# A two-layer streaming encoder step: the dense token group becomes the third and fourth prompt chunk, and its layer-1 keys, values and queries move behind the gathered selection

## The reference

```python
# layer 0 (gMLP mixer), then PEER
h = h + gmlp_mix(rms_norm(h, norm_mix[0]), ...)
h = h + peer_ffn(rms_norm(h, norm_ffn[0]), ...)
kv = rms_norm(h, norm_kv) @ w_kv            # one shared K/V, 4 heads of 64
# layer 1 (windowed attention), then PEER
q = rms_norm(h, norm_mix[1]) @ attn_w_q     # 16 heads of 64
h = h + prompt_or_cached_window_attention(q, k, v) @ attn_w_o
h = h + peer_ffn(rms_norm(h, norm_ffn[1]), ...)
y = rms_norm(h, norm_final)
```

## Time and profile before

| | before |
|---|---|
| median of three runs | 3103.03 us |
| profiled execution, its own time | 3099.71 us |
| its span, first to last instruction | 3097.6 us |
| mean granted TensorE clock, share of full | 0.963 |
| PE busy | 2907.3 us, 94% |
| DVE busy | 2439.5 us, 79% |
| POOL busy | 1028.0 us, 33% |
| ACT busy | 797.2 us, 26% |
| chain that ended last: share of DMA, DVE, PE | 22%, 9%, 5% |

### The profile page before, as it was taken

How to read it: one execution, slowest core, us unless ns; L and a number is a source line. 1 busy time by engine, 2 the same in 40 slices (tenths; PEclk the granted TensorE clock), 3 DMA queues, 4 the chain that set the end, 5 groups by cost and what they waited for, 6 DMA issues and landing times. The chain is left out here.

```text
span 3097.6 us, 46546 instructions
## 1 busy us (share of the span) xinstructions
PE 2907.3 (94%) x17342; PEld 2551.9 (82%) x17342; DVE 2439.5 (79%) x5311; ACT 797.2 (26%) x2328; POOL 1028.0 (33%) x837
## 2 busy tenths in 40 slices
PE   8899899999999999987888979999999999999977
PEld 7898789888888888876677958789888888888856
DVE  3387899988888888877653868998888888888877
ACT  5333222221111211111454352222121221122112
POOL 5532222332233333333365311222233333333332
PEclk9999999999999999998989969989999999999999
DMA  5337889999999999999522358788999999999997
GB/s 182 116 97 288 311 318 365 389 422 422 422 422 422 413 420 413 422 410 416 206 67 83 101 206 309 291 301 335 422 422 421 421 422 419 419 412 420 409 422 292
DMA packets 159964, 1042.97 MB, mean 337 GB/s; under 512 B 18480, under 2 KB 23920, under 8 KB 44096
## 3 DMA queue, kind: packets, MB, share of 16 engines
q0 software_dynamic: 92160, 671.13, 53.0%
q1 hardware_dynamic: 63648, 357.59, 29.8%
q10 hardware_dynamic: 4000, 12.36, 1.0%
HBM read 1033.28 MB, written 7.86 MB: 336 GB/s over the span
## 5 line engine op out<-in xcount | busy, mean ns | idle before, releaser
L779 PE MATMUL bank<-a,V 128*128 128x256 f32 x4096 | 927.8, 386 | 64.4 <-DVE a L1777 56.6
L779 PEld LDWEIGHTS bank<-a,V 128*128 128x128 f32 x4096 | 791.3, 194 | 184.3 <-issue 62.4
L766 PE MATMUL bank<-xd,U 128*128 128x256 f32 x4096 | 935.2, 388 | 3.2 <-DMA U<-uvd 3.2
L1398 POOL DMA_INDIRECT gata<-uvg,idxg x428 | 512.3, 1197 | 1219.6 <-DVE acc L1794 1165.3
L766 PEld LDWEIGHTS bank<-xd,U 128*128 128x128 f32 x4096 | 786.6, 194 | 110.4 <-DMA U<-uvd 4.2
L1786 DVE CUSTOM_DVE_ANT_0 gata<-gata,xrow 128x1024 f32<-128x1024 f32 x428 | 522.6, 1221 | 218.5 <-DMA gata<-uvg,idxg 215.7
L1184 ACT ACTIVATE act<-dot 128x1 f32<-128x1 f32 x640 | 129.6, 202 | 1666.1 <-DVE dot L1786 1666.0
L1794 DVE SCALAR_TENSOR_TENSOR acc<-gata,wgt,acc 128x1024 f32<-128x1024 f32 x428 | 548.1, 1281 | 2.5 <-ACT wgt L1186 2.3
L1398 POOL DMA_INDIRECT gatb<-uvg,idxg x212 | 246.1, 1161 | 531.5 <-DVE acc L1794 521.5
L1786 DVE CUSTOM_DVE_ANT_0 gatb<-gatb,xrow 128x1024 f32<-128x1024 f32 x212 | 259.1, 1222 | 114.7 <-DMA gatb<-uvg,idxg 114.0
L753 PEld LDWEIGHTS bank<-B,oneA 128*128 128x128 f16 x4096 | 278.7, 150 | 32.7 <-issue 19.5
(11 more groups left out here) (207 smaller groups left out, 2482.4 us busy)
## 6 DMA issues: line engine op xcount, KB each, us to landing
U<-uvd SPq DMA_DIRECT2D x128, 1024.0 KB, 9.0
V<-uvd SPq DMA_DIRECT2D x128, 1024.0 KB, 9.0
raw<-lin SPq DMA_DIRECT2D x152, 512.0 KB, 3.6
gata<-uvg,idxg POOLq DMA_INDIRECT x428, 14.7
hsp<-h ACTq DMA_DIRECT2D x2, 2304.0 KB, 17.0
hx<-hsp SPq DMA_DIRECT2D x2, 2304.0 KB, 17.2
gatb<-uvg,idxg POOLq DMA_INDIRECT x212, 14.7
sk_g<-skT ACTq DMA_DIRECT2D x2, 1024.0 KB, 4.8
```

Source lines behind the costliest of these rows:

```text
L766: mm = pe.matmul(bank[s][:, TD * t:TD * t + TD], U[:, s, o:o + P], xd[:, k, :], start=(t == 0 and k == 0), stop=(k == DT - 1), skip_group_ ...
L779: mm = pe.matmul(bank[b][:, TD * (d % 2):TD * (d % 2) + TD], V[:, s, o:o + P], a[:, s, TD * k:TD * k + TD], start=(first and k == 0 and d ...
L1398: pool.indirect_dma_start(row(l, s), None, uvg[l], bass.IndirectOffsetOnAxis(idxg[:, s:s + 1], 0)).then_inc(g_in[s % SLOTS], 16)
```

## The change

On the host the prompt is rolled, so that the dense group now holds prompt tokens 256 to 511 and the gathered group prompt tokens 0 to 255 and the stream. g's attention then needs only g's keys: its chunk 2 is the first of the prompt and has one block. d's chunk 0 now follows g's chunk 3 and has two blocks, as chunk 1 has.

- All that concerns d in layer 1 ahead of its attention moves behind the gathered selection: `n3d`'s sums go behind `n3g`'s, its squares and root behind g's on ACT; the normed keys' operand (`xkv`) is made by DVE in pieces inside the selection `pq1g`; `kvd` follows `pq1g`, then the gathered index, two tiles of `qd` and d's values. The other six tiles of `qd` stand inside d's attention, after units 1, 3, 5, 7, 9 and 11 (`Q_AT`).
- d's attention writes to one PSUM bank instead of two, because the query tiles take bank 5; its results go to buffers of their own (`xo`).
- `n3g`'s scale stays in a PSUM bank, and the second apply of that norm (`mix1`, for the queries) has buffers of its own (`xf2`, `xh2`, `xl2`); it follows the first apply at once instead of waiting until `kvg` is done.
- ACT makes the four high parts of `kvg`'s weights ahead of `n3g`'s squares. The loads of the cached keys move from ACT's queue to SP's, ahead of `qg`'s weights. `kvg`'s low parts stand ahead of the activations' on POOL.
- In `AT`, the four places in d's attention take three gather steps each instead of two: `EARLY[1]` is 62, so that 42 steps instead of 46 are left for the last 16 pairs.

```diff
-    [*[(f"att{n}", 2) for n in (3, 7, 11, 16)], *[(f"add{m}", 1) for m in range(7)], ("mid1", 4),
+    [*[(f"att{n}", 3) for n in (3, 7, 11, 16)], *[(f"add{m}", 1) for m in range(7)], ("mid1", 4),
...
-LOADS = ["ing", "outg", "pq0g", "ind", "outd", "pq0d", "kvd", "kvg", "qg", "og", "pq1g", "qd", "od", "pq1d"]
+LOADS = ["ing", "outg", "pq0g", "ind", "outd", "pq0d", "kvg", "qg", "og", "pq1g", "kvd", "qd", "od", "pq1d"]
...
-IN_BANK = ("n0g", "n0d", "n1g", "n2g", "n4g")
...
+IN_BANK = ("n0g", "n0d", "n1g", "n2g", "n3g", "n4g")
...
+        Q_AT = {2 * m - 3: m for m in range(2, DT)}
...
         def keys(c):
 
-            return (P, [P]) if c == 0 else (0, [P, P]) if c < 4 else (0, [P, DEC])
+            return (P, [P]) if c == 2 else (0, [P, P]) if c < 4 else (0, [P, DEC])
+
+        def out_place(grp, n):
+
+            return (4 + n % 2, n // 2) if grp == "g" else (4, n)
...
+        def tile_bank(name, m):
+
+            if name != "qd":
+                return m % 4, BASE[name][m % 4] + m // 4
+            if m < 2:
+                return 2 + m, BASE["qd"][2 + m]
+            return 5, BASE["qx"][5] + m - 2
...
+            linear("kvg")
+            sp.wait_ge(hsum_done, DT)
+            sp.dma_start(ck[:, :, :], ckT).then_inc(attn_in, 16)
+            sp.dma_start(cvs[:, :], cv).then_inc(attn_in, 16)
+            sp.dma_start(dst[:, :], dist).then_inc(attn_in, 16)
+            sp.dma_start(snk[:, :], sinks.broadcast_to([P, HEADS])).then_inc(attn_in, 16)
...
+                if not l:
+                    norm_sums("n3d")
...
             for m in range(4):
-                tile("kvd", m, None, xd, (nv_done, DT * APPLY["kvd"]))
-            for m in range(4):
                 tile("kvg", m, "kv")
             for m in range(DT):
                 tile("qg", m, "mix1")
...
                     q = qT[grp][r, j, span(grp, c)]
-                    if c == 0:
-                        blocks = [kvs[r, j // 4, 0:P]]
+                    if c == 2:
+                        blocks = [kvs[r, j // 4, k0:k0 + P]]
+                    elif c == 0:
+                        blocks = [kvs[r, j // 4, TCO[3]:TCO[3] + P], kvs[r, j // 4, 0:P]]
...
                     if n < len(UNITS[grp]):
+                        if grp == "d" and n % 2 == 0:
+                            pe.wait_ge(*tile_out("qd", n // 2))
                         att_scores(grp, n)
                     if 0 <= n - LAG < len(UNITS[grp]):
                         att_turn(grp, n - LAG)
                     if 0 <= n - LAG - 1:
                         att_out(grp, n - LAG - 1)
-                for b in (4, 5):
-                    pe.wait_ge(free[b], BASE[f"att{grp}"][b] + len(UNITS[grp]) // 2)
+                    if grp == "d" and n in Q_AT:
+                        tile_d("qd", Q_AT[n], xd)
...
             selection(1, "g")
-            for m in range(DT):
-                tile("qd", m, None, xd, (nv_done, DT * APPLY["mix1d"]))
-                if m == 4:
-                    second_rank(1, 0)
-                if m == 5:
-                    gathered_index(1, 0, (0,))
-                if m == 6:
-                    gathered_index(1, 0, (1,))
+            for m in range(4):
+                tile_d("kvd", m, xkv, (nv_done, DT * APPLY["kvd"]))
+            second_rank(1, 0)
+            gathered_index(1, 0, (0,))
+            gathered_index(1, 0, (1,))
+            for m in range(2):
+                tile_d("qd", m, xd, (nv_done, DT * APPLY["mix1d"]))
+            values("d")
+            pe.wait_ge(vnat_done, 4)
             attention("d")
...
+                if l:
+                    root("n5d")
...
+            for m in range(4):
+                weight_high("kvg", m)
             squares_of_sums(0)
             for dt in range(DT):
-                act.wait_ge(nv_done, DT * APPLY["kvd"] + dt + 1 + (dt % 2 == 0))
-                act.activation(h[:, dt, COLS["d"]], dense_sum(dt), ACT.Copy).then_inc(dsum_done, 1)
-                if dt % 2 == 1:
-                    act.wait_ge(dsum_done, dt + 1)
-                    act.nop().then_inc(free[4 + dt // 2], 1)
-
-            act.dma_start(ck[:, :, :], ckT).then_inc(attn_in, 16)
-            act.dma_start(cvs[:, :], cv).then_inc(attn_in, 16)
-            act.dma_start(dst[:, :], dist).then_inc(attn_in, 16)
-            act.dma_start(snk[:, :], sinks.broadcast_to([P, HEADS])).then_inc(attn_in, 16)
+                square("n3d", h[:, dt, COLS["d"]], dt)
             high_parts("kv", "kvg")
...
+            root("n3d")
...
-            high_parts("mix1", "mix1g")
...
+                if m < 2:
+                    high_parts("mix1", "mix1g", range(4 * m, 4 * m + 4))
...
                 else:
-                    act.activation(xd[:, j, span(grp, c)], bank[b][:, 0:TCS[c]], ACT.Copy).then_inc(free[b], 1)
+                    act.activation(xo[j][:, span(grp, c)], bank[b][:, 0:TCS[c]], ACT.Copy).then_inc(free[b], 1)
...
                         weights_at(1, f"att{n}")
+                        if n in Q_AT:
+                            query("d", Q_AT[n])
...
-            queries("d")
+            for m in range(4):
+                act.wait_ge(*tile_done("kvd", m))
+                act.activation(kvs[:, m, COLS["d"]], bank[m][:, 0:TD], ACT.Copy).then_inc(free[m], 1)
+                if m == 2:
+                    gate_exp(1, 0)
...
+            for m in range(2):
+                query("d", m)
...
+            act.nop().then_inc(vnat_done, 1)
             attention("d")
...
+            first_lows("kvg")
             low_parts(PARTS["kv"])
-            first_lows("kvg")
-            first_lows("qg")
-            low_parts(PARTS["mix1"])
+            for m in range(4):
+                first_lows("qg", (m,))
+                if m < 2:
+                    for dt in (4 * m, 4 * m + 2):
+                        low_part(pool, PARTS["mix1"], dt, xl_done)
...
+                    elif l and 3 <= m < 3 + DT:
+                        keys_d([m - 3])
...
+                    if l and dt == 1:
+                        inverse("n5d")
+                    if l and dt >= 2:
+                        dense_out([dt - 2])
+                if l:
+                    dense_out(range(DT - 2, DT))
...
+            def keys_d(pieces):
+
+                dve.wait_ge(xr_done, 2)
+                apply(G_KV, "d", lambda dt: h[:, dt, COLS["d"]], lambda dt: xkv[:, dt, :], pieces=pieces)
...
-            normed("n3g", G_KV, "g", "kv")
-            for b in range(4):
-                dve.wait_ge(*tile_done("kvg", b))
-            normed(None, G_MIX1, "g", "mix1")
...
+            inverse("n3g")
+            of_h = lambda dt: h[:, dt, COLS["g"]]
+            apply(G_KV, "g", of_h, lambda dt: xf[:, dt, :], "kv", norm="n3g", keep=True)
+            apply(G_MIX1, "g", of_h, lambda dt: xf2[:, dt, :], "mix1", norm="n3g")
+            inverse("n3d")
...
+    x = np.concatenate([f["x_prompt"][0, TD:], f["x_prompt"][0, :TD], f["x_sample"][0]])
```

More of the change, by code:

```diff
@@ L148, in plan @@
     chosen_g(1)
-    lin("qd")
-    seg("attd", **{f"b{b}": 8 for b in range(8)})
+    lin("kvd")
+    seg("vnd", b4=1, b5=1)
+    seg("qd", b2=1, b3=1)
+    seg("qx", b5=6)
+    seg("attd", b0=8, b1=8, b2=8, b3=8, b4=16, b6=8, b7=8)
     lin("od")
@@ L403, in wait_slot @@
                 eng.wait_ge(lo_done[m % 4], LO[last] + k // 4 + 1)
-            elif name == "kvd":
+            elif name == "kvg":
                 for b in range(2):
@@ L1006, in squares_of_h, with high_parts @@
                 root(norm)
-            def high_parts(part, ap):
-                for dt in range(DT):
+            def high_parts(part, ap, pieces=range(DT)):
+                f, hi = (xf2, xh2) if part == "mix1" else (xf, xh)
+                for dt in pieces:
                     act.wait_ge(nv_done, DT * APPLY[ap] + dt + 1)
-                    act.activation(xh[:, dt, :], xf[:, dt, :], ACT.Copy).then_inc(xh_done, 1)
+                    act.activation(hi[:, dt, :], f[:, dt, :], ACT.Copy).then_inc(xh_done, 1)
             def gate_tile(grp, m):
@@ L1363, in _ @@
             selection(1, "g")
-            queries("d")
+            for m in range(4):
[3 more added lines that the diff above has]
+                    gate_exp(1, 0)
+            for b in range(4):
+                act.wait_ge(*tile_out("kvd", b))
+            act.dma_start(kvT, kvs[:, :, P:2 * P]).then_inc(out_done, 16)
+            for m in range(2):
+                query("d", m)
+            for k, c in enumerate(DC):
+                b, n = values_bank("d", k)
+                act.wait_ge(full[b], n + 1)
+                act.activation(vnat[0:TCS[c], c, :], bank[b][0:TCS[c], 0:KVH * DH], ACT.Copy).then_inc(free[b], 1)
+            for k in range(len(DC)):
+                b, n = values_bank("d", k)
+                act.wait_ge(free[b], n + 1)
+            act.nop().then_inc(vnat_done, 1)
             attention("d")
@@ L1491, in release, with apply @@
                 dve.nop().then_inc(free[NBANK[name]], 1)
```

(4 more changed lines are left out.)

160 lines of the change are left out of this document (88 added, 72 removed).

## The result

The changed kernel took 3119.19 us (median of six runs, 3115.90 to 3122.20), the kernel before 3103.49 (six runs): a ratio of 1.0050, with a 95% interval of 1.0040 to 1.0061. It is slower by 15.7 us, just outside the top of the range that was given. The profiled execution is the slowest of the six: 3122.20 us, span 3120.4. It lies 22.5 us above the profiled execution before (3099.71), so the profiles overstate the change by some 7 us.

The account below looks back on a forecast made before the run. Transfers were taken to bound the late part, waits between engines in serial stages the part before 2136 us. -13 - 5.3 + 2.7 + 28 - 9.9 = +2.5 gave 3102.2 us profiled, 3105.5 on the median; range 3089 to 3119.

Parts of the forecast that it names:

- (b): g's attention: one-block units save 0.66 us per period, eight times, -5.3 us; bounds 0 and -8.
- (a): End of layer 0 to g's attention: earlier `kvg`, no wait behind it, work removed; -13 us, between -5 and -18.
- (c): Selection to end of d's attention: +30.7 us, of which +2.7 before that attention and +28 inside it.
- some 20: Sign that the forecast was right: the gathered index ready some 20 us earlier.
- (d): Last 16 pairs: four more early gathers leave 42 for 46, at 2.49 us each, -9.9 us; other bound 0.
- The clock stays low in d's attention: Rival: in d's attention query tiles take 7 us, rounds 24.6, +41.5 instead of +28; 3119 us; chance 0.20.
- The clock holds: Rival: d's attention at full clock takes 76.4 us (+19.9), with (a) at -16; total 3094 us; chance 0.36.
- The four gathers buy nothing: Rival: PE becomes the bound in the last 16 pairs, so (d) is 0; 3115.5 us; chance 0.07.

Follow-up runs that it names:

- e5: Changed kernel, PE alone given the missing half of each one-block unit in g's attention (scores, transpose, output nobody reads): 3101.95 us.
- e8: Kernel before, with the gathered group's first chunk given one key block instead of two: 3112.61 us, ratio 1.0024.
- e4: Changed kernel with the six query tiles ahead of d's attention instead of inside it: 3133.83 us.
- e3: Changed kernel with two gather steps instead of three at the four places in d's attention: 3112.86 us.
- e6: Changed kernel with e5's unread PE work and two gather steps per place instead of three: 3099.09 us, ratio to the kernel before 0.9981.
- e7: e6 plus twelve matmuls of no use in the first gap of g's attention: 3099.05 us, ratio to the kernel before 0.9981.
- e9: Changed kernel with two gather steps per place and, of e5's unread work, only the second block's scores: 3106.57 us, from 3103.54 to 3119.03.
- e11: e7 without the second output: unread scores and transposes, two gather steps, twelve matmuls in the first gap: 3100.21 us, ratio to the kernel before 0.9988.
- e1: Changed kernel with the gathered group's first prompt chunk given two real key blocks again: 3108.53 us, runs from 3103.9 to 3118.5.

## Why the prediction was wrong

**The step that failed is (b)**, "I take 0.66 per period", with its bounds of 0 and -8. It counted what a one-block unit takes from DVE, and bounded the gain by POOL's pace. Neither sets the period: in e5 both have their one-block work, the clock is 1.00, and the period is still 6.77. The term had no upward bound, though the change takes half of PE's work off one unit of three, in a stage whose mean clock of 0.92 was made of a slow start and a steady 1.00. The clock was priced for d's attention alone. What the runs showed in its place: PE, with less to do, stays at 0.50, becomes the bound at 8.47 us a period, and the stage takes 71.6 us instead of 60.5. e8 and e5 show the cause from both sides: taking the block away in the old kernel costs 10 us in this stage, giving PE the missing work back in the new one wins 12. With +11.2 in place of -5.3 the sum would have been +19.0; the medians moved by 15.7, the profiles by 22.5. Why PE's share of a two-block unit is enough for the clock and that of a one-block unit is not stays open.

**(a)**, -13 forecast, was -15.9: the first key tile came at 1521.60 instead of 1529.55, 8 us earlier against 4 (in the experiments in the new order it began between 1519.95 and 1525.13), and no idle time of PE stands between the key tiles and the queries of g. The queries' second apply had been timed right, its wait is gone.

**(c)** held in its sum. The way from og to d's attention got 1.3 us longer (2.7 forecast). The first gather left at 1783.49 instead of 1790.77: 7 us earlier and not the "some 20" of the signs, since g's attention had lost 11. d's attention took 84.7 (84.5), and that match is luck: its parts were off by some 12 us each way (e4), and the third step costs 2.8 to 3.25 (e3) where 2.35 was put.

**(d)** was mis-sized: four early gathers were to win 9.9. The experts' stage is 1046 to 1050 us in the six profiled runs with three steps, and 1054.6 to 1056.4 in the five with two (e3, e6, e7, e9, e11): a difference near 7. Why 4 x 2.49 did not come back whole is open: from 2800 to 3080 us the DMA share is 0.99 to 1.01 in the changed kernel too. The steps' price in d's attention, 11 to 13 us, was not worth it: e3 is 6 us faster than the changed kernel, and e6 with two steps is no slower than e5 with three.

**The rivals.** "The clock stays low in d's attention" gave 3119, and that is what was measured, but not for its reason. d's attention was at a mean clock of 0.84 and took 84.7 us, not 98. That the number fits is luck. The low clock came in another stage, for which the same view stood in the earlier trace rows. The Trainium skill's rule on the clock, from the page "TensorE: Matmul & The Clock Gate", section "HAM oscillation", tells of waits that cost the clock. The trace agrees for d's attention (empty at 1807 to 1811, slow behind it). In g's attention the clock falls in a wait too, but no wait is left to blame for its staying low: PE is busy 62.55 of 64 us at 0.50, and more work, not fewer waits, ended it. "The clock holds" would have needed g's attention to hold it too. "The four gathers buy nothing" is refuted, at 7 of 9.9.

Small slips in the prediction's sums (+19.5 for +19.9 as the lower end of d's attention, 98 for 98.4, 3115.5 for 3115.4) change nothing.

## What to carry to other kernels

A change that takes matmul work out of a stage with waits can cost more than the work was worth: read the stage's clock in short windows first, and ask whether what is left held 1.00 anywhere in the trace. If the clock is 0.50 and PE is busy all through, try adding matmuls that nobody reads before removing anything: here that gave back 17 us, where the removed work was to win 5.3 and at most 8. And a gather step placed in a chain of engines can cost more than its own length: here 2.8 to 3.25 us for a step of 2.35.

## What the runs showed that was not expected

PE can be busy almost without a pause and stay at 0.50: 62.55 of 64 us in the changed kernel, and 9.9 of every 10 us from 1595 to 1635 in e8. Matmuls that nobody reads made the changed kernel 17.2 us faster (e5). And there is an in-between: with only the scores added (e9), the same program took from 3103.5 to 3119.0 us over twelve runs, and the faster runs were those with the higher mean clock. e1, with two real blocks, spreads almost as far.
